# Two joined transformer blocks on one core: the first block's output product token tile by token tile, angles computed earlier, modulation rows added on VectorE

## The reference

```
# first block (one layer)
shift, scale, gate = split(silu(c) @ w_ada + b_ada)          # 3 x 1024 columns
u = layer_norm(x) * (1 + scale) + shift
proj = u @ w_in + b_in                                       # 12 sections of 1024 columns
y_a, y_b, y_c = pooling, short convolution, 31-tap convolution branches of proj
m = sum_i sigmoid(merge_i) * (y_i @ w_branch[i])             # three branches
x = layer_norm(2**0.25 * x + gate * (m @ w_out), ln_g, ln_b)
# second block (two layers): rotary tables from positions (cos, sin), then per layer
h = rms_norm(x, norm_mix); q, k, v, gates = split(h @ w_in_2)
x = x + mixed_attention(q, k, v, gates) @ w_out_2
x = x + conv_ffn(rms_norm(x, norm_ffn)) @ w_down_2
out = rms_norm(x, norm_final)
```

## Time and profile before

| | |
|---|---|
| median of 3 runs | 2204.77 us (2204.25 to 2207.14) |
| the profiled execution's own time | 2204.68 us |
| its span | 2202.9 us |
| TensorE busy | 2169.7 us (98%) |
| VectorE busy | 1253.3 us (57%) |
| ScalarE busy | 773.4 us (35%) |
| mean DMA rate | 99 GB/s |

### The profile page before, as it was taken

The page is one execution under the profiler, slowest core; times in us unless marked ns, Lnnn a source line. Parts: engine busy times, 40 slices in busy tenths (PEclk is TensorE's granted clock), DMA queues, the critical chain, the costliest instruction groups (busy, mean ns, idle before and its releaser), DMA issues.

```text
span 2202.9 us, 25712 instructions
## 1 busy us (share of the span) xinstructions
PE 2169.7 (98%) x10775; PEld 1804.6 (82%) x10775; DVE 1253.3 (57%) x1611; ACT 773.4 (35%) x1022; POOL 25.7 (1%) x42
## 2 busy tenths in 40 slices
PE   6999999999999899999999999999999999999998
PEld 3888888888888788987888888889898788888887
DVE  5898797953663847433855554234743475555422
ACT  2323232223353245344343333135434434333321
POOL 1000000000000000000000000000000000000000
PEclk9999999999999999999999999999999999999999
DMA  8432322333223122322223222322232222222322
GB/s 294 141 105 90 115 82 96 100 111 99 95 90 125 60 96 77 116 77 73 87 73 113 96 96 96 105 67 96 77 116 77 77 96 77 96 96 97 106 94 77
DMA packets 184151, 217.92 MB, mean 99 GB/s; under 512 B 3804, under 2 KB 159076, under 8 KB 184036
## 3 DMA queue, kind: packets, MB, share of 16 engines
q1 hardware_dynamic: 180048, 210.52, 28.8%
q10 hardware_dynamic: 3252, 3.60, 0.5%
q0 software_dynamic: 736, 2.15, 0.3%
HBM read 212.06 MB, written 4.19 MB: 98 GB/s over the span
## 4 chain that ended last, share of the span: by engine, by line
PE 94%; DVE 3%; ACT 1%; issue 1%; DMA 1%; POOL 0%; SPq 0%; POOLq 0%; ACTq 0%; DVEq 0%
PE psum L1640 30%; PE psum L1641 29%; PE psum L1642 29%; PE psum L1914 1%; PE psum L1945 1%; PE psum L1748 1%; PE psum L1977 1%; PE psum L1957 1%; DVE whl L475 1%; DMA ada<-in_w_ada 1%; DVE hT L1342 0%; PE psum L1901 0%; PE psum L1930 0%; POOL stat L620 0%; ACT hT L808 0%
## 5 line engine op out<-in xcount | busy, mean ns | idle before, releaser
L1640 PE MATMUL psum<-hT,whl 128*128 128x512 f32 (+1 forms) x2112 | 802.7, 380 | 7.7 <-DVE hT L1342 5.5
L1642 PE MATMUL psum<-hT,whl 128*128 128x512 f32 (+1 forms) x2112 | 795.9, 377 | 0.0
L1641 PE MATMUL psum<-hT,whl 128*128 128x512 f32 (+1 forms) x2112 | 795.9, 377 | 0.0
L475 DVE TENSOR_TENSOR whl<-raw,whl 128x1024 fp32r<-128x1024 f32 (+1 forms) x368 | 446.9, 1216 | 456.4 <-ACT whl L468 456.3
L468 ACT ACTIVATE whl<-raw 128x1024 fp32r<-128x1024 f32 (+1 forms) x368 | 384.2, 1047 | 445.6 <-PE psum L1642 430.8
L1640 PEld LDWEIGHTS psum<-hT,whl 128*128 128x128 f32 x2112 | 398.4, 189 | 89.0 <-issue 11.3
L1642 PEld LDWEIGHTS psum<-hT,whl 128*128 128x128 f32 x2112 | 398.3, 189 | 73.0
L1641 PEld LDWEIGHTS psum<-hT,whl 128*128 128x128 f32 x2112 | 398.6, 189 | 71.5 <-issue 0.5
L1640 PE MATMUL psum<-whl,ff 128*128 128x512 f32 x352 | 137.1, 389 | 0.0
L1642 PE MATMUL psum<-whl,ff 128*128 128x512 f32 x352 | 136.9, 389 | 0.0
L1641 PE MATMUL psum<-whl,ff 128*128 128x512 f32 x352 | 136.9, 389 | 0.0
(11 more groups left out here) (278 smaller groups left out, 2146.2 us busy)
## 6 DMA issues: line engine op xcount, KB each, us to landing
raw<-in_w_in SPq DMA_DIRECT2D x88, 1024.0 KB, 5.1
raw<-in_w_up SPq DMA_DIRECT2D x44, 1024.0 KB, 5.1
raw<-in_w_down SPq DMA_DIRECT2D x20, 1024.0 KB, 5.0
ada<-in_w_ada SPq DMA_DIRECT2D x12, 1024.0 KB, 14.3
raw<-in_w_branch SPq DMA_DIRECT2D x12, 1024.0 KB, 5.1
raw<-in_w_out SPq DMA_DIRECT2D x12, 1024.0 KB, 5.1
x<-in_x SPq DMA_DIRECT2D x4, 512.0 KB, 7.3
v_by_token<-vnat ACTq DMA_DIRECT2D x4, 512.0 KB, 2.9
```

The costliest lines, as they stand in the source:

```text
L475: nc.vector.tensor_tensor(whl_view(w, 1), raw_view(w), whl_view(w, 0).bitcast(F), ALU.subtract).then_inc(w_lo, 1)
L1640: M(out_, stat_hi, mov_hi, start=start, stop=False, **kw)
L1641: M(out_, stat_hi, mov_lo, start=False, stop=False, **kw)
L1642: return M(out_, stat_lo, mov_hi, start=False, stop=stop, **kw)
```

## The change

The change has three parts.

**Setup.** TensorE takes k tiles 0 to 2 of rows 0 to 2 and 0 to 4 of row 3 (`PE_ROWS`), VectorE the rest; VectorE then adds TensorE's row from PSUM to one partition of its own sum, so ScalarE's `arow` copies and half of the matmuls in `ada_columns` are gone. TensorE's order is columns 0, product 2, columns 1, product 3, columns 2 and 3. The loads of `cstage` and `gaterow` move behind `split_hi(1)` on ScalarE's queue, and the two casts from `cstage` behind the modulated input on VectorE.

**Angles.** `pos_i` is loaded when the second branch is summed; the angle steps stand in steps 2 to 5 of the third branch on VectorE, in other places of the buffer; the sines run right behind the splits of w_out, and a copy puts the first into `table` later.

**Output product.** All eight pieces of w_out are held at once (`apart` gives four of them places in the working area), and TensorE runs token tile by token tile, both halves of a tile one after the other in banks 2tb and 2tb+1, with the transposes of token tiles 0 and 1 behind the fifth and the seventh product tile. `room_for` says what each piece's split waits for. VectorE and ScalarE follow in a new order, and the rows of ln_g and ln_b are loaded behind the last chunk of w_out.

```diff
+    PE_ROWS = (3, 3, 3, 5)
+    ada_rows = lambda b, k: ada[:, 2 * b + k // 4, k % 4 * SEQ:(k % 4 + 1) * SEQ]
+    w_first = W[("w_out", None, 0, 0)]
+    apart = {w_first + i: over(f"apart{i}", at_ * K, [P, 2, 1024], R) for i, at_ in ((3, 0), (4, 48), (5, 56), (7, 88))}
...
+            slot = (w_first + 3 if w == w_first + 6 else w) % 4
...
+        def room_for(w):
+            i = w - w_first
+            last = W[("w_branch", 2, 7)] + 1
+            if i == 3:
+                nc.scalar.wait_ge(w_used, W[("w_branch", 1, 7)] + 1)
+                nc.scalar.wait_ge(s_rt, 2)
+            elif i in (4, 5, 6):
+                nc.scalar.wait_ge(w_used, last)
+            elif i == 7:
+                nc.scalar.wait_ge(m_lo, KT)
+            elif i in (8, 9, 10):
+                nc.scalar.wait_ge(w_used, w - 7)
+            elif i == 11:
+                nc.scalar.wait_ge(w_used, w - 4)
+            elif w >= 4:
+                nc.scalar.wait_ge(w_used, w - 3)
...
@@ SyncE
-                if chunks[c][0] == "w_out" and chunks[c - 1][0] != "w_out":
-                    w_wait_full(sp, ("w_branch", 1, 7))
+                if chunks[c][1] == ("w_branch", 2, 1):
+                    sp.wait_ge(m_part, KT)
+                    sp.dma_start(pos_i[:], t["positions_2"].to_broadcast((P, SEQ))).then_inc(s_pos, 16)
+                if chunks[c - 1][0] == "w_out" and chunks[c][0] != "w_out":
+                    w_wait_full(sp, ("w_branch", 2, 7))
                     sp.dma_start(lnrow[:, 0, :], t["ln_g"].to_broadcast((P, D))).then_inc(s_ln, 16)
                     sp.dma_start(lnrow[:, 1, :], t["ln_b"].to_broadcast((P, D))).then_inc(s_ln, 16)
-                    sp.dma_start(pos_i[:], t["positions_2"].to_broadcast((P, SEQ))).then_inc(s_pos, 16)
@@ ScalarE
-            act.dma_start(cstage[:], t["consts"][:, NKEEP:NCONST]).then_inc(s_cst, 16)
-            act.dma_start(gaterow, t["b_ada"][:, 2048:3072].to_broadcast((P, D))).then_inc(s_bcast, 16)
-            ada_row(0)
...
-            for b in range(1, TB):
-                ada_row(b)
             split_hi(0)
             split_hi(1)
+            act.dma_start(cstage[:], t["consts"][:, NKEEP:NCONST]).then_inc(s_cst2, 16)
+            act.dma_start(gaterow, t["b_ada"][:, 2048:3072].to_broadcast((P, D))).then_inc(s_bcast, 16)
...
+            split_hi(w_first + 3)
             mixture_hi(KT - 1)
+            for i in range(4, 8):
+                split_hi(w_first + i)
+            act.wait_ge(s_rt, 2)
+            A(rt[:, 0, :], rt[:, 0, :], ACT.Sin).then_inc(s_sin, 1)
+            A(rt[:, 1, :], rt[:, 1, :], ACT.Sin).then_inc(s_tab, 1)
...
                 norm_sum(s, 0)
                 scaled(s, 0)
-                norm_sum(s, 1)
-                scaled(s, 1)
                 if s == 2:
+                    norm_sum(s, 1)
+                    norm_hi(s, 0)
+                    scaled(s, 1)
                     split_hi(w0 + 4)
-                    norm_hi(s, 0)
+                    split_hi(w0 + 5)
+                    split_hi(w0 + 6)
+                    norm_sum(s, 2)
                     norm_hi(s, 1)
-                    split_hi(w0 + 5)
-                    norm_sum(s, 2)
-                    split_hi(w0 + 6)
                     split_hi(w0 + 7)
                     scaled(s, 2)
                     norm_sum(s, 3)
                     norm_hi(s, 2)
                     scaled(s, 3)
+                    act.wait_ge(s_sin, 1)
+                    act.wait_ge(row_read, 8)
+                    A(table[:, 0, :], rt[:, 0, :], ACT.Copy).then_inc(s_tab, 1)
@@ VectorE
-                weighted(adsum[:, 2 * b:2 * b + 2, :].rearrange("p a b -> p (a b)"),
-                         lambda k: ada[:, 2 * b + 1, (k - 4) * SEQ:(k - 3) * SEQ], range(4, KT)).then_inc(s_adsum, 1)
+                part = adsum[:, 2 * b:2 * b + 2, :].rearrange("p a b -> p (a b)")
+                weighted(part, lambda k: ada_rows(b, k), range(PE_ROWS[b], KT)).then_inc(s_part, 1)
+                dve.wait_ge(s_part, b + 1)
+                dve.wait_ge(arow_ps, b + 1)
+                own = part[32 * b:32 * b + 1, :]
+                V.tensor_tensor(own, own, bank(7)[32 * b:32 * b + 1, :], ALU.add).then_inc(s_adsum, 1)
...
+                        if i == 2 and m == 7:
+                            split_lo(w_first + 3)
...
+                        if i == 2 and m == 2:
+                            angles()
+                            whole_turns(0.25)
+                        if i == 2 and m == 3:
+                            reduced(0, 0.25)
+                        if i == 2 and m == 4:
+                            whole_turns(0.0)
+                        if i == 2 and m == 5:
+                            reduced(1, 0.0)
...
+            for i in range(4, 8):
+                split_lo(w_first + i)
             dve.wait_ge(s_ln, 32)
-            row_splits(first, 0)
-            for tb in range(TB):
-                first_rows(0, tb)
-                if tb == 0:
-                    row_splits(first, 1)
             w0 = resident(first)
+            first_rows(0, 0)
             first_rows(1, 0)
             first_normed(0)
+            first_rows(0, 1)
             first_rows(1, 1, 0)
             first_normed(1)
+            first_rows(0, 2)
+            gained(2, 0)
+            norm_lo(2, 0)
             first_rows(1, 2, 1)
-            gained(2, 0)
+            first_normed(2)
             split_lo(w0 + 4)
+            split_lo(w0 + 5)
+            first_rows(0, 3)
+            split_lo(w0 + 6)
             gained(2, 1)
-            norm_lo(2, 0)
             norm_lo(2, 1)
-            first_normed(2)
-            split_lo(w0 + 5)
             first_rows(1, 3, 2)
-            split_lo(w0 + 6)
+            split_lo(w0 + 7)
             first_normed(3)
@@ TensorE
-                pe.wait_ge(arow_in, b + 1)
                 pe.wait_ge(s_adsum, b + 1)
                 for m in range(4):
-                    M(o_, arow[0:1, b, m * P:(m + 1) * P], negones[0:1, 0:1], start=True, stop=False)
-                    ins = M(o_, adsum[:, 2 * b + m // 2, m % 2 * P:(m % 2 + 1) * P], negones[:, 0:1], start=False, stop=True)
+                    ins = M(bank(6)[:, 4 * b + m:4 * b + m + 1], adsum[:, 2 * b + m // 2, m % 2 * P:(m % 2 + 1) * P], negones[:, 0:1],
+                            start=True, stop=True)
...
-            row_tiles(ROWS[0], lambda k: mhi[:, k, :], lambda k: mlo[:, k, :], (m_lo, 0))
+            for tb in range(TB):
+                ts = slice(tb * P, (tb + 1) * P)
+                for half in range(2):
+                    b = 2 * tb + half
+                    take(b)
+                    for k0 in range(0, KT, 2):
+                        w = W[("w_out", None, half, k0)]
+                        pe.wait_ge(w_lo, w + 1)
+                        hi, lo = whl_view(w, 0), whl_view(w, 1)
+                        for kk in range(2):
+                            k = k0 + kk
+                            if b == 0:
+                                pe.wait_ge(m_lo, k + 1)
+                            ins = passes(bank(b), mhi[:, k, ts], mlo[:, k, ts], hi[:, kk, :], lo[:, kk, :], k == 0, k == KT - 1)
+                        if tb == 3:
+                            ins.then_inc(w_used, 1)
+                    if tb < 3:
+                        ins.then_inc(row_full, 1)
+                    give(b, row_read, row_reads(ROWS[0], half, tb))
+                    if b in (4, 6):
+                        transposed(2, b // 2 - 2)
```

More of the change, by code:

```diff
@@ L295, in build @@
     mlo = over("mlo", 32 * K, [P, KT, SEQ], R)
-    lnrow = over("lnrow", 0, [P, 2, D])
+    lnrow = over("lnrow", 24 * K, [P, 2, D])
     prod = over("prod", 8 * K, [P, 2, SEQ])
-    pos_i = over("pos_i", 12 * K, [P, SEQ], I32)
-    ang = over("ang", 14 * K, [P, SEQ])
-    rt = over("rt", 16 * K, [P, 3, SEQ])
+    pos_i = over("pos_i", o + 16384, [P, SEQ], I32)
+    ang = over("ang", o + 16384, [P, SEQ])
+    turns = over("turns", 0, [P, SEQ])
+    rt = over("rt", 12 * K, [P, 2, SEQ])
+    w_first = W[("w_out", None, 0, 0)]
+    apart = {w_first + i: over(f"apart{i}", at_ * K, [P, 2, 1024], R) for i, at_ in ((3, 0), (4, 48), (5, 56), (7, 88))}
     qd = over("qd", 0, [P, 3, 2, SEQ])
@@ L508, in row_wait @@
             name, l, nk = stage
-            if tb < 3:
+            if l is None and tb < 3:
+                eng.wait_ge(row_full, 2 * tb + half + 1)
+            elif tb < 3:
                 eng.wait_ge(row_full, ROWS.index(stage) * 6 + half * 3 + tb + 1)
@@ L516, in row_reads @@
             i = ROWS.index(stage)
-            return 4 * half + tb + 1 if i == 0 else 8 + 4 * (i - 1) + tb + 1
+            return 2 * tb + half + 1 if i == 0 else 8 + 4 * (i - 1) + tb + 1
         def proj_wait(eng, s_full, name, l, j, mm):
@@ L1351, in first_rows @@
                 xs = x[:, tb, half * 512:(half + 1) * 512]
-                if half or tb >= 2:
-                    dve.wait_ge(dve_chain, x_part[half if tb >= 2 else 0, (tb - 2) % TB])
```

(20 more changed lines are left out.)

101 lines of the change are left out of this document (48 added, 53 removed).

## The result

The changed kernel took 2192.2 us (median of 4, 2191.76 to 2193.3), the kernel before 2204.53 us in the same comparison (median of 4): a ratio of 0.9942, 95% interval 0.9925 to 0.9959. The forecast was 2191.3 us. The profiled execution took 2193.30 us for a span of 2191.5; against the one of before that is 11.4 us less.

What follows compares the result with a forecast made beforehand. TensorE, busy 94% of the 2202.9 us span, was taken as the bound, so only its idle or small work could be had. 2202.9 - 8.5 (setup) - 4.9 (border) = 2189.5, with 1.8 around it 2191.3 us; range 2187.0 to 2197.5.

Steps and rivals of the forecast that it cites:

- The setup: Start of the kernel up to the first hT: modulation and ScalarE's splits end sooner, gaining 8.5 us.
- (d): Setup loads: cstage and gaterow moved behind split_hi(1) bring the last w_ada piece 2.2 us sooner, at 33.0.
- Rival A: Setup: w_ada pieces come no sooner, or VectorE becomes the bound; setup gains 6.3, total 2193.5 us; chance 0.17.
- (b): Setup on VectorE: new product shares plus adding TensorE's PSUM row at 0.7 us; rows cost 4.3, 4.3, 4.3, 2.75 us.
- (a): Setup on TensorE: each set of one-column products halves to 1.5 us, at most 2.4; one set stays in the path.
- ScalarE's release: Setup: after chunk 0 at 35.7, two splits (1.99 us) and two load issues (about 0.4 each) end at 38.6.
- The clock: Setup handover: full speed would give 1.5 us more; forecast wrong if it falls earlier and stays low longer after 38.6.
- The angles and the first token tile: Third branch and start of w_out's product: moved angles and pieces 4 to 7 cost nothing, splits in time by 0.9 to 1.6 us.
- Rival D: Output product: the fourth w_out chunk comes late, one for one from 1.4 us; about 19 us late gives 2209.1; chance 0.04.
- The tail: Border of the two blocks: second half of the first tiles starts at 782.9 instead of 787.83, gaining 4.9 us.
- the other term, 3.8: Border: if the clock falls behind the 2.9 us idle, sq 0 ends 2.2 later, 1.1 hidden, so the gain is 3.8.
- Rival B: Border gives nothing: VectorE is busy throughout and a reorder only moves the idle; 2196.2 us; chance 0.14.

Runs made afterwards that it cites:

- e1: Kernel before with only the setup's edits (row shares, addition on VectorE, moved loads, TensorE's order): 2194.79 us, ratio 0.9948 to the kernel before.
- e2: Changed kernel with the loads of cstage and gaterow back at the head of ScalarE's queue: 2194.76 us.
- e8: Changed kernel with the eight transposes behind the modulation done three times over, to keep TensorE busy before its first product: 2190.77 us.
- e10: Changed kernel with both the border's new VectorE, ScalarE and TensorE order and the setup's repeated transposes: 2187.39 us, ratio 0.9916 to the kernel before.
- e5: Changed kernel with the eighteen angle instructions back between the third branch and w_out's splits, scratch row elsewhere: 2204.03 us, ratio 0.9987 to the kernel before.
- e6: Changed kernel with the load of the last w_out chunk held until piece 5 is split: 2199.47 us.
- e4: Changed kernel with twelve unused 512-column matmuls on TensorE between the last product tile and the second block's first product: 2192.02 us.
- e3: Changed kernel with the border reordered: earlier mean squares, gained(1) and norm_lo(1) before splits 9 and 10, earlier transposes, scaled(2) before split 11: 2190.23 us.

## Why the prediction was right, step by step

**The setup, 8.5 forecast, 8.6 found** at the third branch's end (9.1 to 9.2 in e1).
- The moved loads (d): the last piece was forecast at 33.0 and came at 33.10; e2 shows the cause. Rival A is out.
- The addition (b): forecast 0.7 for want of a row, measured 0.69 for one partition of 512 words. Row 3 was forecast to end at 35.8 and ended at 35.88.
- The one-column products (a): 1.1 us a set for 1.5. The 2.9 a set of before held slow records; the size was off by 0.4 and hidden behind ScalarE.
- ScalarE's release: forecast 38.6, found 38.01. Chunk 0 came 0.4 later than forecast (36.1), but the DMA issues, counted as 0.8 behind the splits, ran beside the first of them.
- The clock was named as what could go wrong. It stayed low for 5.3 us after the first product (40.44 to 45.7) where it had been 3.5, and takes back 0.8 of the 9.4 us that stood at the first product. The small errors and this one cancel: about 0.9 us came more than forecast up to the first product and 0.8 was lost behind it, so that 8.5 fits 8.6 is partly luck. e8 shows that TensorE's idle of 1.9 us prolonged the stretch, not that it began it: with the idle filled the clock fell in e8's profile and did not in e10's.

**The angles and the first token tile** were costed at nothing. TensorE ran from the third branch to its last w_out product without idle. Splits ended at 718.7 (forecast 727.3, less 8.6), the lnrow loads held nobody. e5 and e6 show that both covers are real: without the first it costs 10.3 us by the trace; beyond the margin of the second, forecast as 1.4 and found 1.3 to 1.4, it costs more than one for one (6.5 us for a split 6.3 later, of which the margin took 1.3). Rival D had its mechanism right and its price too low, for the forecast left out the clock.

**The tail, 4.9 forecast, 4.3 found.** norm_lo(1) was forecast for 767.6, less 8.6, and ended at 758.99, the same; the idle 2.9, found 2.83. The sum took 4.9, which holds only if the clock stays up. It fell, as the other term, 3.8, had it: twelve and more matmuls at 0.21. So this step of the sum was wrong in its choice and 0.6 too high. The fall was also mis-sized: e4 puts it at about half a microsecond, not 1.1. The section "HAM oscillation — how this bites in real kernels" of the Trainium skill's page "TensorE: Matmul & The Clock Gate", to which the prediction ties the 3.8, tells of longer waits for loads than this one; it is the trace that shows the fall behind 2.83 us. Rival B, a border that gives nothing, is out by the 4.3 us, and its reason, that VectorE's amount of work keeps the idle whatever the order, by e3.

**The sum.** 8.6 and 4.3 are 12.9 us at the second block's second half, against the 13.4 forecast. The profiled execution lost 1.5 of it at 1040 to 1060. With the median's 12.3 us, 2191.3 was 0.9 low; the forecast had no term for this loss, and could have none from the profile of before. What stays open is that fall at 1040 to 1060: it stands in both profiles of the changed kernel and in those of e3 and e5 to e8, and not in those of before, e1, e2, e4 and e10, with TensorE busy throughout. No experiment was made on it, so its cause is not known. The same holds for the fall between 1740 and 1780, in every profile but e8's.

## What to carry to other kernels

An idle of a few microseconds on TensorE has two prices: the idle, and the matmuls behind it at half clock. Here they were 4.8 and 1.7 us; filling the idle with harmless work pays a little where nothing else is late (1.5 us at the handover, 0.4 to 0.6 at the border, by the traces). A gain of 1 to 2 us in the medians may be a fall of the clock that happened to be missing elsewhere; comparing the same instruction in both traces tells them apart. A load that nobody needs yet, issued ahead of loads on the critical path, costs its bytes over the full DMA rate even from another engine's queue (0.83 MB, 2.2 us). And an order that wants all weights at once is only as good as what stands in front of their splits: the same token-tile order is worth 4.3 us, or loses 6.0, with eighteen small instructions in one place or the other.

## What the runs showed of the hardware

- The granted clock fell after 2.83 us of idle on TensorE, and did not after 1.3. In the changed kernel it then stayed low until about 762.6, 3.4 us; in e2, after the same idle, until past 766:

```profile
764.00:766.00 2.00, 2.00 (x11) 2.00 (x11) 2.00 (x3) 0.62 (x1) 0.78 (x1) 0.50 0.00 0
766.00:768.00 2.00, 2.00 (x15) 2.00 (x15) 1.07 (x2) 1.15 (x2) 0.00 (x0) 0.74 0.62 169
```

  So the price of one and the same idle differed by over 1 us from one profile to another.
- The clock can fall while TensorE is busy 100% of the time (0.91 over 1040 to 1060; 0.91 over 1760 to 1780 in the profile of before), in some profiles and not in others; the part of the program that runs there is the same in all. Each such fall took 1.5 us.
- A DMA issue on ScalarE's queue stood at 36.10 beside the activation that starts at 36.10: issues between activations were free here.
- A tensor_tensor over one partition of 512 words took 0.69 us, as much as over 128 partitions.
